# A two-block transformer step on one core: work moved between engines in the SSD mixer, the start and the block change

## The reference

```python
def reference(x, mem, ...):
    x = first_block(x, mem, ...)      # 2 layers, then rms_norm
    return second_block(x, ...)       # 2 layers

# a layer of the first block
x = x + hybrid_mixer(rms_norm(x), ...)          # neighbourhood attention and grouped attention
x = x + memory_cross_attention(rms_norm(x), rms_norm(mem), ...)
x = x + conv_ffn(rms_norm(x), ...)

# a layer of the second block
x = x + 0.5 * swiglu(rms_norm(x), ...)
z, xbc, dt_raw, q, k, v = split(rms_norm(x) @ w_in)
xbc = silu(causal_depthwise_conv(xbc))
y_ssd = ssd_mixer(xbc, dt_raw, z, ...)
y_att = dilated_attention(rms_norm(q), rms_norm(k), v)     # 16 heads of 64
x = x + concatenate([y_ssd, y_att]) @ w_out
x = x + 0.5 * swiglu(rms_norm(x), ...)
```

## Time and profile before

| | us |
|---|---|
| median of three runs | 2026.6 |
| lowest, highest | 2025.88, 2027.09 |
| profiled execution, its own time | 2026.03 |
| its span, first to last instruction | 2024.2 |
| TensorE, VectorE, ScalarE, GpSimd busy | 1964.3, 1326.1, 1094.6, 210.1 |
| mean granted TensorE clock | 0.997 |

### The profile page before, as it was taken

One profiled execution on the slowest core, in us unless ns is written; L12 is line 12 of the kernel. 1 busy time (PEld: TensorE's weight loads), 2 busy tenths in 40 slices (PEclk: granted clock), 3 DMA queues, 4 the chain that ended last, 5 costly groups with the idle time before them and its releaser, 6 DMA issues.

```text
span 2024.2 us, 30515 instructions
## 1 busy us (share of the span) xinstructions
PE 1964.3 (97%) x12072; PEld 1720.0 (85%) x12072; DVE 1326.1 (66%) x2316; ACT 1094.6 (54%) x1862; POOL 210.1 (10%) x240
## 2 busy tenths in 40 slices
PE   6999999999999999999998999999999999999999
PEld 6878998887899978889986788888888997778887
DVE  5767976576697665555676875555555576786554
ACT  5666765465676554445556454444444565545442
POOL 1231121033112100000024000000000012200000
PEclk9999999999999999999999999999999999999999
DMA  6434556543455646555442255555555453235553
GB/s 256 136 119 128 191 185 232 174 132 112 135 181 182 202 158 199 186 182 173 150 147 95 84 168 192 181 184 185 189 181 188 148 165 126 86 105 188 187 182 128
DMA packets 90110, 329.92 MB, mean 163 GB/s; under 512 B 9968, under 2 KB 10352, under 8 KB 89584
## 3 DMA queue, kind: packets, MB, share of 16 engines
q1 hardware_dynamic: 89968, 327.97, 49.3%
HBM read 326.88 MB, written 1.05 MB: 162 GB/s over the span
## 4 chain that ended last, share of the span: by engine, by line
PE 82%; DVE 7%; ACT 5%; issue 2%; POOL 1%; ACTq 0%; DVEq 0%
PE PS L83 79%; PE PS L86 3%; ACT WH L92 2%; DVE WL L98 2%; DVE TMP L108 1%; ACT TMP L95 1%; DVE SM L114 1%; ACT TMP L94 1%; DVE TMP L98 1%; ACT TMP L92 1%; DVE TMP L105 0%; DVE SM L108 0%; DVE SM L98 0%; POOL SQ L111 0%; POOL M L104 0%
## 5 line engine op out<-in xcount | busy, mean ns | idle before, releaser
L98 DVE TENSOR_TENSOR WL<-RAW,WH 128x1024 fp32r<-128x1024 f32 x608 | 745.8, 1232 | 533.2 <-ACT WH L92 526.6
L92 ACT ACTIVATE WH<-RAW 128x1024 fp32r<-128x1024 f32 x608 | 640.8, 1058 | 542.4 <-PE PS L83 537.2
L83 PE MATMUL PS<-WH,GH 128*128 128x512 f32 (+1 forms) x912 | 361.4, 396 | 3.6 <-DVE WL L98 2.4
L83 PE MATMUL PS<-WL,GH 128*128 128x512 f32 (+1 forms) x912 | 353.8, 388 | 0.0
L83 PE MATMUL PS<-WH,GL 128*128 128x512 f32 (+1 forms) x912 | 353.6, 388 | 0.0
L83 PE MATMUL PS<-GH,WH 128*128 128x256 f32 x1104 | 316.4, 287 | 1.0 <-issue 0.4
L83 PE MATMUL PS<-GH,WL 128*128 128x256 f32 x1104 | 312.6, 283 | 0.0
L83 PE MATMUL PS<-GL,WH 128*128 128x256 f32 x1104 | 312.6, 283 | 0.0
L83 PE MATMUL PS<-WH,HH 128*128 128x512 f32 (+1 forms) x736 | 279.0, 379 | 0.0
L83 PE MATMUL PS<-WH,HL 128*128 128x512 f32 (+1 forms) x736 | 276.5, 376 | 0.0
L83 PE MATMUL PS<-WL,HH 128*128 128x512 f32 (+1 forms) x736 | 276.4, 376 | 0.0
(11 more groups left out here) (143 smaller groups left out, 2388.4 us busy)
## 6 DMA issues: line engine op xcount, KB each, us to landing
RAW<-wts SPq DMA_DIRECT2D x608, 512.0 KB, 4.1
M<-bias SPq DMA_DIRECT2D x2, 2048.0 KB, 13.5
X<-x SPq DMA_DIRECT2D x2, 512.0 KB, 6.1
TMP<-mem SPq DMA_DIRECT2D x1, 1024.0 KB, 12.4
out<-X SPq DMA_DIRECT2D x4, 256.0 KB, 3.4
CST<-cst SPq DMA_DIRECT2D x1, 706.0 KB, 10.4
M<-gf SPq DMA_DIRECT2D x1, 512.0 KB, 5.1
PAR<-par SPq DMA_DIRECT2D x1, 368.0 KB, 7.5
```

The costliest lines, as they stand in the source:

```text
L83: return Issued(self.eng and self.eng.matmul(o, l, r, start=first, stop=last, skip_group_check=share))
L92: return Issued(self.eng.activation(o, i, f, scale=scale))
L98: return Issued(self.eng and self.eng.tensor_tensor(o, a, b, op))
```

## The change

It does eight things.
1. Start: the gains (first 32 columns of PAR) are loaded by themselves ahead of half 0, the other parameters behind half 2; the bias comes in four pieces behind halves 5 to 8. A copy of one element runs first on ScalarE. ScalarE makes two tiles of HH, splits half 0, makes two more, splits half 1, makes tiles 4 to 7, then splits 2 and 3, and takes the squares of x; half 4 and the squares of mem follow before q is copied out. VectorE follows that order; halves 5 and 6 are split around the scaling of mem. FG is computed after the first layer's block.
2. Change of blocks: the two products with the gain follow both updates (`gained_x`), the second ones with their squares within the swiglu, and `final_norm` runs at steps 4 and 6 of the first gate group.
3. swiglu: the fifth group is turned and split at step 6 instead of 3.
4. Decays: cum is computed once more, transposed (16 heads on partitions, 256 tokens; each half of the tokens has its own matmul), split into a high part (partitions 0 to 15) and a low part (32 to 47) in CUM, which shares memory with WDH and WDL. HEAD is two identity matrices of 16 on the same partitions. `decay(h)` is one split-format matmul of HEAD's column h, repeated 128 times, with CUM's 256 columns.
5. Turning: `xd` and `cb` are a second generator, `prepared`, beaten in the attention at PREP_RATES on TensorE and VectorE. The z tiles 0 and 1 and the outputs of the last four pairs are held to fewer banks.
6. Scan on ScalarE: fill beats stand ahead of the decays.
7. Gate: `y_gate` leaves VectorE; GpSimd multiplies by Z behind its divisions.
8. The arrangement of signals follows (gain_in, gated).

```diff
@@ build
-        WDH = sb("WDH", [128, 128], FR)
-        WDL = sb("WDL", [128, 128], FR)
+        WDHL = sb("WDHL", [128, 256], FR)
+        WDH, WDL = WDHL[:, 0:128], WDHL[:, 128:256]
+        CUM = WDHL[0:48, :]
+        HEAD = sb("HEAD", [48, 16], FR)
+        PREP_RATES = [0, 0, 0] + [0, 1, 0] + [1, 1, 0] + [0, 0, 0] + [1, 0, 0] * 5
+        def hidden_at(b):
+            return 6 if b == 5 else 3
@@ pe_program
-                        ob = take((a, "o", i), OB + STB if a[0] == "dil" and i >= 4 else OB)
+                        ob = take((a, "o", i), OB)
...
                         fill.beat(next(rate))
+                        if prep is not None:
+                            prep.beat(PREP_RATES[3 * i + u])
...
-                        if b >= 1 and i == 3:
+                        if b >= 1 and i == hidden_at(b):
                             turn_hidden(b - 1)
@@ pe_program, dt_sums
+                    ps = take(("cumt", L), WHOLE)
+                    for t in range(2):
+                        for o in (0, 32):
+                            m = e.mm(ps[o:o + 16, t * 128:t * 128 + 128], ADT[:, t * 16:t * 16 + 16], cc(C_CA, 128), True,
+                                     True)
+                    m.then_inc(ssd, ("cumt", L))
@@ pe_program, block2
-                        fm_tile(("z", L, m), whole, WT)
+                        fm_tile(("z", L, m), whole, WT if m >= 2 else (0, 1))
+                def prepared():
+                    for b in range(4):
+                        ps = take(("xd", L, b), (0, 1) if b < 3 else STB)
+                        for q in range(2):
+                            e.wait_ge(ready, ("xc", L, 2 * b + q))
+                            for t in range(2):
+                                m = e.turn(ps[:, t * 256 + q * 128:t * 256 + q * 128 + 128],
+                                           XC[:, 2 * b + q, t * 128:t * 128 + 128], ident)
+                        m.then_inc(ssd, ("xd", L, b))
+                        yield
+                    for g in range(4):
+                        ps = take(("cb", L, g), STB)
...
                 def decay(h):
                     ps = take(("dec", L, h), (4, 5))
-                    for t in range(2):
-                        m = e.mm(t_cols(ps, t), ADT[:, t * 16 + h:t * 16 + h + 1].to_broadcast([128, 128]),
-                                 cc(C_CA, 128), True, True)
-                    m.then_inc(ssd, ("dec", L, h))
+                    e.wait_ge(made, "head")
+                    e.wait_ge(dout, ("cumt", L))
+                    e.mm(ps[:, 0:256], HEAD[:, h:h + 1].to_broadcast([48, 128]), CUM, True, True).then_inc(
+                        ssd, ("dec", L, h))
@@ act_program
                 if L == 0:
+                    for k in range(4):
+                        high_x(("mix", 0), k, col(P_MIX + k), 0)
+                        if k == 1:
+                            highs_to(0)
                     highs_to(1)
-                    for k in range(4):
+                    for k in range(4, 8):
                         high_x(("mix", 0), k, col(P_MIX + k), 0)
                     highs_to(3)
                     for c in range(2):
                         squares(("mix", 0), c, lambda c, t: (x_in[c], 0))
-                    for k in range(4, 8):
-                        high_x(("mix", 0), k, col(P_MIX + k), 0)
...
+                    if n == 16:
+                        e.wait_ge(ssd, ("cumt", L))
+                        for o in (0, 32):
+                            i = e.act(ACT.Copy, CUM[o:o + 16, :], bank(("cumt", L))[o:o + 16, 0:256])
+                        i.then_inc(ready, ("cumt", L))
...
+                fill.beat(1)
                 decay(0)
                 decay(1)
-                fill.beat(1)
                 for p in range(8):
+                    fill.beat(SSD_RATE)
                     if p < 7:
                         decay(2 * p + 2)
                         decay(2 * p + 3)
                     if p >= 2:
                         y_square(p - 2)
-                    fill.beat(SSD_RATE)
...
+            e.wait_ge(made, "begun")
+            e.act(ACT.Copy, SS[:, 13:14], SS[:, 12:13])
+            e.wait_ge(gain_in, 0)
@@ dve_program
                 if L == 0:
-                    lows_to(1)
                     for k in range(4):
                         low_x(("mix", 0), k, gain(k), 0)
-                    lows_to(3)
+                        if k == 1:
+                            lows_to(0)
+                    lows_to(1)
                     for k in range(4, 8):
                         low_x(("mix", 0), k, gain(k), 0)
+                    lows_to(3)
                     norm(("mix", 0))
+                    lows_to(4)
+                    e.wait_ge(squared, ("mem", 1, 1))
+                    mean_square(8)
+                    y = newton(2)
+                    e.copy(RM, y).then_inc(small)
+                    e.wait_ge(small)
+                    for t in range(2):
+                        lows_to(5 + t)
+                        e.ts(MEMT[:, t, :], MEMT[:, t, :], RM[:, t:t + 1], None, ALU.mult).then_inc(made, ("mem", t))
...
                 if final:
-                    final_norm((f, L))
+                    gained_x(1)
...
+                        if final and b == 0 and i == 4:
+                            final_norm((f, L))
+                        if final and b == 0 and i == 6:
+                            final_norm_end((f, L))
+                            e.wait_ge(small)
...
                         y_skip(p - 1)
-                        y_gate(p - 1)
@@ pool_program
                 divide(("dil", L), 16, [128, 256])
+                for m in range(8):
+                    y = XC[:, m, :]
+                    e.wait_ge(dout, ("z", L, m))
+                    e.wait_ge(dout, ("y", L, m))
+                    e.tt(y, y, Z[:, m, :], ALU.mult).then_inc(gated, ("yz", L, m))
@@ sp_program
+            e.dma(PAR[:, 0:P_CW], par[:, 0:P_CW]).then_inc(gain_in, 0)
             half(0)
-            e.dma(PAR[:, :], par).then_inc(par_in, 0)
...
+            e.dma(PAR[:, P_CW:P_N], par[:, P_CW:P_N]).then_inc(par_in, 0)
...
-            e.dma(BIAS, bias[0, :, :, :]).then_inc(bias_in, 0)
             for h in range(RAWS, 2 * UNITS):
                 half(h)
+                if h < RAWS + 4:
+                    q = 2 * (h - RAWS)
+                    e.dma(BIAS[:, q:q + 2, :], bias[0, :, q:q + 2, :]).then_inc(bias_in, 0)
```

More of the change, by code:

```diff
@@ L548, in run, with attention @@
                     pass
-            def attention(a, heads, widths, fill, rates, two=True):
+            def attention(a, heads, widths, fill, rates, two=True, prep=None):
                 n, rate = len(heads) // 2, iter(rates)
@@ L1085, in block1 @@
                                   acc=SS[:, 8 + 2 * t + c:9 + 2 * t + c]).then_inc(squared, ("mem", c, t))
+                else:
+                    rest_of_x(("mix", 1), lambda k: col(pb + P_MIX + k), side, ("nq", 1, 0))
+                for m in range(4):
+                    out(NQ[:, m, :], ("nq", L, m))
+                highs(("nk", L, 0))
                 highs(("nk", L, 1))
@@ L1234, in conv_c, with swiglu @@
                 return conv_t(n)[:, 260:516]
-            def swiglu(f, L, side, gain, then=()):
+            def swiglu(f, L, side, gain, then=(), final=False):
                 def hidden(b):
@@ L1355, in block2 @@
                 run(dilated)
-                for b in range(8):
-                    fill.beat(XD_RATE)
                 def decay(h):
@@ L1366, in y_square @@
                 def y_square(m):
[L1367 removed]
+                    e.wait_ge(gated, ("yz", L, m))
                     if m >= 4:
@@ L1608, in attention @@
                         inverse(2 * i + 1)
-                    for _ in range(3):
+                    for u in range(3):
                         fill.beat(next(rate))
+                        if prep is not None:
+                            prep.beat(PREP_RATES[3 * i + u])
                 low(n - 1)
@@ L1643, in block1 @@
                 key_tile(0)
-                if L == 0:
-                    e.wait_ge(squared, ("mem", 1, 1))
-                    mean_square(8)
-                    y = newton(2)
-                    e.copy(RM, y).then_inc(small)
-                    e.wait_ge(small)
-                    for t in range(2):
-                        e.ts(MEMT[:, t, :], MEMT[:, t, :], RM[:, t:t + 1], None, ALU.mult).then_inc(made, ("mem", t))
                 lows(("nk", L, 1))
@@ L1885, in block2 @@
                 even(("wmix2", L), 0)
+                if L == 0:
+                    e.copy(HEAD[:, :], CST[0:48, C_HD:C_HD + 16]).then_inc(made, "head")
                 e.wait_ge(ready, ("wdh", L))
@@ L1977, in block2 @@
                         dt_sums()
+                    if n == 18:
+                        e.wait_ge(ready, ("cumt", L))
+                        e.tt(CUM[32:48, :], bank(("cumt", L))[32:48, 0:256], CUM[32:48, :].bitcast(F32),
```

(25 more changed lines are left out.)

110 lines of the change are left out of this document (43 added, 67 removed).

## The result

The changed kernel took **1989.61 us** (median, 1989.35 to 1990.06) against 2026.43 us of the kernel before in the same runs: a ratio of 0.9818, 95% interval 0.9801 to 0.9835. The forecast was 1995.2 us, range 1986 to 2009. The profiled execution took 1990.06 us, 36.0 less than that of before (2026.03), where the sum said 31.4.

A forecast was written before the change was run, and what follows sets the result against it. TensorE, busy 97% of the span, was taken as the bound. Savings of 3.3 + 4.1 + 3.6 + 5.6 + 14.8 = 31.4 us from 2026.0 gave 1994.6 profiled, 1995.2 median; range 1986 to 2009.

The forecast's parts named there:

- The start: Start of the run: first weight matmul 4.1 us earlier, 2.8 given back in waits, 2.0 from mem's turn; 3.3 us saved.
- Change of blocks: Between the blocks: TensorE's 2.40 us wait and the half clock's 1.7 us loss both go; 4.1 us saved.
- swiglus: At four ends of gate matmuls, turning the fifth hidden group later removes stops of 0.9 us each; 3.6 us saved.
- Turning in attention: Mixed layers: 4.3 us of turning fills attention's idle time, 1.4 not covered; 2.8 a layer, 5.6 us saved.
- signs of being wrong: Attention idle time up over 3 us a layer, scan halves over 1.6 us, or half clock stretches in new places.
- Decays: Scan: eight pairs' decays fall from 8.0 to 3.2 us of TensorE's work, 4.8 a layer, net 3.9.
- Order and gate: Scan: ScalarE's split first and the gate off VectorE save 1.8 us of idle time and 1.7 of clock a layer.
- Transposed sums: Mixed layers: eight new TensorE instructions on 128 columns for the transposed sums cost 0.9 us a layer.
- Rival (a): VectorE becomes the bound: attention gains nothing from turning, the scan gains half; 2008 us, chance 0.2.
- (b): Scan: GpSimd's gates exclude VectorE's work, each adding 0.85 us on its path; 13.6 us back, 2009, chance 0.05.
- (c): A cycle in attention through a turning step's bank loses 2.4 us a pair; 2039 us, chance 0.04.
- (d): Start and change of blocks do nothing, as DMA or the norm ends last; 7.4 us lost, 2002.6, chance 0.06.

The follow-up runs named there:

- the run with steps in holes: Changed kernel with one turning step in each of six pairs from the third on, two in the last, some in other banks; 1987.65 us, ratio 0.9814.
- the run with the later steps: Changed kernel with turning steps starting in the third pair, z tiles 0 and 1 allowed any of three banks; 2007.98 us, ratio 0.9914.
- decays alone: Kernel before plus only the transposed sums and split-matmul decays, with ScalarE's order and the gate as they were; 2025.83 us, ratio 1.0002.
- the order alone: Kernel before with only ScalarE's fill beats in the scan moved ahead of the decays; 2017.8 us, ratio 0.9961.
- order back: Changed kernel with ScalarE's fill beats in the scan put behind the decays again; 2008.5 us, ratio 0.9916.
- the one with the turning behind: Changed kernel with the turning of inputs put behind the attention again; 1996.55 us, ratio 0.9858.

## Why the prediction was right, and where not

- **The start**: right in size (3.6 for 3.3) by two deviations that cancel, and within the 2 us by which executions differ there. The first matmul came 4.8 us earlier instead of 4.1. The waits for low parts gave back 2.85, where 2.8 was taken. The turn of mem no longer waits, but a new wait of 0.90 behind it leaves 1.5 of its 2.0.
- **Change of blocks and swiglus**: right. Idle time and half clock both went; the four swiglus won 1.0 each for 0.9.
- **Turning in attention**: right in kind. Two of three early steps do cost 0.7 us each (1.4 forecast; 1.51 and 1.36 measured), and the steps from the fourth pair on are hidden. That this cost belongs to where those two steps stand, and not to VectorE's load as such, is shown by the run with steps in holes, which has the same work (two of its steps also use other banks). The outputs' second bank was indeed not missed; another bank would have been (the run with the later steps). One of the prediction's own signs of being wrong did come: stretches at half clock in new places, two in attention. They cost 0.2 us at most there.
- **Decays**: "8.0 - 3.2 = 4.8 a layer" was a price of TensorE's own work, added whatever the order. That step is wrong: it is 0.1 without the new order (decays alone), and with it, over the scan, 3.9 (8.33 - 4.45, the gate on VectorE, with the turning moved too) or 2.8 (8.57 - 5.78, the gate on GpSimd), to which the first pair's decays add 0.5. The price of 0.4 for a pair was right: 0.43 us from one pair's decays to the next fill. What keeps the rest from showing was not tested; VectorE has 42.9 us of work in those 46.9.
- **Order and gate**: forecast 3.5 a layer, measured 4.45 for the order alone and 0.24 for the gate. The earlier trace rows had the cycle in sight: ScalarE's 2.75 us of waiting recurs each pair, and its length is given by VectorE. I read it as slack of ScalarE and took only TensorE's 2.1 us of idle time for what it costs. TensorE's busy time had hidden this: its long decays filled the wait, and with short ones in the same 55.0 us (order back) it is busy 48.1. That the total of the scan came out right is luck: the decays, too dear by 1 to 2, and the order, too cheap by 1, make up for each other once both are in.
- **Transposed sums**: "0.9 us" for eight instructions was near (0.64 measured at their place), but the step missed that VectorE's small operation breaks up two halves that held GpSimd off: +0.9 became -0.86. This is the 3.5 us.
- **Rival (a)**, VectorE becomes the bound: true in a small part, 0.66 a step in two places of attention. **(b)**, the gates exclude VectorE: the mechanism is real (below), its price is not, since most of the waiting is GpSimd's own, and TensorE never waits for the gate (ScalarE does at the scan's end, 3.0 us in two times, against 2.3 with the gate on VectorE). **(c)** did not occur; that waits for banks can be as dear as it feared, the run with the later steps shows (3.1 and 5.5 us in the first layer). **(d)** is out.

What stays open: why the tiles around the sums win a further 0.37 us a layer, what bounds the scan now, and what decides where a stretch at half clock falls.

## What to carry to other kernels

When a stage has a steady period, follow one period through the engines' timelines and add the steps that release each other before pricing any edit: here 2.72 + 1.44 + 1.08 = 5.24 us ran over VectorE and ScalarE alone, so 4.8 us less of TensorE's work was worth nothing until one instruction left that chain, and TensorE's 52.9 busy of 55.0 us did not tell. Such a cycle holds only while the engine outside it stays faster: one stretch at half clock brought TensorE back in. Work that is moved into gaps is to be placed by the engine that is full there and by the banks it holds: the same steps cost 1.4 us a layer, 0.1 or 10.8. Try parts of a change both alone and left out: 4.45 and 0.15 made 8.33.

## What the hardware showed that I had not expected

**GpSimd and VectorE take turns here**, by whole instructions as far as these rows show. The first of GpSimd's key-scale copies, each 0.29 us when nothing is in its way, took 2.35 while VectorE did two halves in a row. In the scan of the changed kernel GpSimd's gates show it too (timeline of GpSimd):

```profile
1115.17 0.74 POOL L98 TENSOR_TENSOR M<-M 128x256 f32<-128x256 f32 x1 [14.83 <-DVE M L108]
1119.43 2.60 POOL L98 TENSOR_TENSOR M<-M 128x256 f32<-128x256 f32 x1 [3.52 <-DVE M L108]
```

VectorE's rows beside the second (half, then two products, all with two inputs in SBUF, then an operation out of PSUM):

```profile
1119.28 1.21 DVE L98 TENSOR_TENSOR WL<-RAW,WH 128x1024 fp32r<-128x1024 f32 x1
1120.41 1.01 DVE L98 TENSOR_TENSOR TMP<-TMP,M 128x384 f32<-128x384 f32 x2
1121.35 1.11 DVE L105 TENSOR_SCALAR TMP<-PS,SM 128x128 f32<-128x128 f32 x4
```

The gate that started at 1119.43 ends at 1122.03, 0.68 us after VectorE turns to PSUM. The other way round, the half that started 0.10 us after the gate of 1115.17 took 1.73 instead of 1.22. The Trainium skill (GPSIMD Engine Reference, Specifications) says that GpSimd shares its SBUF interfaces with VectorE and contends with instructions that have two SBUF inputs; the traces agree. In the groups of the scan the gates average 1356 ns and the halves 1292, against 424 for a gate on VectorE and 1222 for a half without gates beside it:

```profile
L98 DVE TENSOR_TENSOR WL<-RAW,WH 128x1024 fp32r<-128x1024 f32 x10 | 12.9, 1292 | 0.8 <-ACT WH L92 0.8
L98 POOL TENSOR_TENSOR M<-M 128x256 f32<-128x256 f32 x8 | 10.9, 1356 | 33.8 <-DVE M L108 33.8
```

**Stretches at half clock move.** In them the granted clock is 0.50, the lower of its two levels (1.2 and 2.4 GHz). Nearly all last 3.4 us. Leaving out the last microseconds of each run, the changed kernel has two (1064.6 and 1689.2 us), the two kernels with the same attention but the gate on VectorE or full decays have none, the one with the turning behind has two, the one with later steps five, of which two last 6.8. What TensorE did before the clock fell differs: it was idle for 2.40 us at the change of blocks of the kernel before and for 2.00 in each layer's attention of the changed kernel, but in the first scan of the kernel before for only 0.56, followed by 1.95 us of 16 matmuls of one column. What one costs depends on what TensorE has to do there. In the changed kernel's attention, where TensorE waits for probabilities, it is 0.2 us at most (attention +1.34 to +1.54 in four layers with one, +1.33 to +1.38 in six without, all with the turning steps as in the changed kernel). In attention without turning steps it is 1.0 (+1.01 to +1.04 in four layers with one, 0.01 to 0.06 in four without), and at the change of blocks 1.6, by the two kernels that have the old code there and no stretch.
